# Products with moving weights: columns read in turn from two halves of a weight row

## The reference

```
h = rmsnorm(x, g)                                  # 256 x 1024
proj = h @ w_in                                    # 1024 x 6672, split: q, k, v, gates, ...
mixed = gs0 * (ya @ w_branch_a) + gs1 * (yb @ w_branch_b) + gs2 * (yc @ w_branch_c)
x = x + rmsnorm(mixed @ w_out, g)
f = (silu(h @ w_gate) * (h @ w_up)) @ w_down       # 1024 x 2816, twice, and 2816 x 1024
...                                                # three such feed-forward layers in all,
                                                   # a second mixer, a cross attention to 256 memory rows
```

## Time and profile before

| what | value |
|---|---|
| median of three runs | 1101.3 us (1101.09 to 1101.75) |
| span of the profiled execution | 1100.8 us |
| TensorE matmul busy | 1087.9 us, 99% |
| TensorE weight load busy | 981.1 us, 89% |
| VectorE busy | 719.8 us, 65% |
| ScalarE busy | 555.3 us, 50% |
| DMA, mean over the span | 192 GB/s |

### The profile page before, as it was taken

One profiled execution on the slowest core, in us unless ns is written; L12 is line 12 of the kernel. 1 busy time (PEld: TensorE's weight loads), 2 busy tenths in 40 slices (PEclk: granted clock), 3 DMA queues, 4 the chain that ended last, 5 costly groups with the idle time before them and its releaser, 6 DMA issues.

```text
span 1100.8 us, 18185 instructions
## 1 busy us (share of the span) xinstructions
PE 1087.9 (99%) x7530; PEld 981.1 (89%) x7530; DVE 719.8 (65%) x1085; ACT 555.3 (50%) x840; POOL 30.3 (3%) x49
## 2 busy tenths in 40 slices
PE   9999999999999999999999999999999999999997
PEld 8898878889999988899999889887788989999985
DVE  5687665877666645656666545867767657666653
ACT  6643575545444544544454445646644446445442
POOL 0000500000000000000000001000000000000000
PEclk9999999999999999999999999999999999999999
DMA  7654545655665665576686559534365445565662
GB/s 265 231 173 159 192 148 198 225 188 175 193 204 185 221 200 182 192 248 211 233 274 207 174 186 321 185 113 128 122 235 173 148 133 188 189 202 190 196 203 77
DMA packets 63821, 211.01 MB, mean 192 GB/s; under 512 B 7451, under 2 KB 14803, under 8 KB 62844
## 3 DMA queue, kind: packets, MB, share of 16 engines
q1 hardware_dynamic: 63452, 209.57, 57.6%
q10 hardware_dynamic: 288, 0.29, 0.1%
HBM read 206.41 MB, written 5.27 MB: 192 GB/s over the span
## 4 chain that ended last, share of the span: by engine, by line
PE 85%; DVE 6%; ACT 4%; DMA 3%; issue 1%; POOL 0%; SPq 0%; POOLq 0%; ACTq 0%; DVEq 0%
PE ps L869 13%; PE ps L872 13%; PE ps L871 13%; PE ps L861 12%; PE ps L863 12%; PE ps L862 12%; DMA raw<-in_wflat 3%; DVE wlo L1652 1%; PE ps L911 1%; ACT whi L1313 1%; PE ps L1043 1%; PE ps L958 1%; ACT m_Pb L1463 1%; PE ps L1029 1%; PE ps L1234 1%
## 5 line engine op out<-in xcount | busy, mean ns | idle before, releaser
L869 PE MATMUL ps<-hT_hi,whi_b 128*128 128x256 f32 x1344 | 373.7, 278 | 0.5 <-DVE wlo_b L1652 0.5
L871 PE MATMUL ps<-hT_hi,wlo_b 128*128 128x256 f32 x1344 | 371.2, 276 | 0.0
L872 PE MATMUL ps<-hT_lo,whi_b 128*128 128x256 f32 x1344 | 371.2, 276 | 0.0
L1652 DVE TENSOR_TENSOR wlo<-raw,whi 128x1024 fp32r<-128x1024 f32 x176 | 215.4, 1240 | 113.7 <-ACT whi L1313 112.9
L1652 DVE TENSOR_TENSOR wlo_b<-raw,whi_b 128x1024 fp32r<-128x1024 f32 (+1 forms) x186 | 217.4, 1189 | 106.2 <-ACT whi_b L1313 105.9
L869 PEld LDWEIGHTS ps<-hT_hi,whi_b 128*128 128x128 f32 x1344 | 252.3, 188 | 3.7 <-issue 2.3
L871 PEld LDWEIGHTS ps<-hT_hi,wlo_b 128*128 128x128 f32 x1344 | 252.3, 188 | 0.3
L872 PEld LDWEIGHTS ps<-hT_lo,whi_b 128*128 128x128 f32 x1344 | 252.3, 188 | 0.0
L1313 ACT ACTIVATE whi<-raw 128x1024 fp32r<-128x1024 f32 x176 | 181.9, 1057 | 110.4 <-PE ps L863 89.1
L1313 ACT ACTIVATE whi_b<-raw 128x1024 fp32r<-128x1024 f32 (+1 forms) x186 | 183.2, 1024 | 32.4 <-PE ps L863 15.3
L861 PE MATMUL ps<-whi,hT_hi 128*128 128x512 f32 (+1 forms) x256 | 101.8, 398 | 1.6 <-DVE wlo L1652 1.6
(11 more groups left out here) (338 smaller groups left out, 1317.6 us busy)
## 6 DMA issues: line engine op xcount, KB each, us to landing
raw<-in_wflat SPq DMA_DIRECT2D x355, 512.0 KB, 4.0
wide<-scratch SPq DMA_DIRECT2D x1, 2048.0 KB, 11.2
m_w<-in_cmp_k_w SPq DMA_DIRECT2D x4, 512.0 KB, 6.1
m_w<-in_cmp_v_w SPq DMA_DIRECT2D x4, 512.0 KB, 6.1
m_alibi<-in_c_alibi SPq DMA_DIRECT2D x1, 1536.0 KB, 6.6
m_xT<-in_xT SPq DMA_DIRECT2D x4, 256.0 KB, 5.6
x<-in_x SPq DMA_DIRECT2D x2, 512.0 KB, 8.9
m_memT<-in_memT SPq DMA_DIRECT2D x1, 1024.0 KB, 5.9
```

What stands on the lines that cost most here:

```text
L869: e.matmul(o, hi[:, k, c], xs.h(k0 + k), start=first and k == 0 and f % 2 == 0, stop=False, skip_group_check=True)
L871: e.matmul(o, lo[:, k, c], xs.h(k0 + k), start=False, stop=False, skip_group_check=True)
L872: r = e.matmul(o, hi[:, k, c], xs.l(k0 + k), start=False, stop=last and k == kt - 1, skip_group_check=True)
L1652: e.tensor_tensor(slot(wlo, u)[:, w], raw[u % NRAW][:, w], slot(whi, u)[:, w].bitcast(F32), ALU.subtract).then_inc(*w_lo.did(u, c))
```

## The change

A helper gives an access pattern that reads the first half and the second half of a row in turn: word 0, word n/2, word 1, word n/2 + 1, and so on. All moving weight operands of kind "a" go through it. The host lays the columns of these products out as all even ones and then all odd ones, so that what is read in turn is the original order of columns, and results and evictions stay as they were. Kinds "b" and "s" and everything else are untouched.

```
+        def in_turn(ap):
+            return ap.rearrange("p (a b) -> p b a", a=2)
...
-                            e.matmul(o, xh, hi[:, k, :], start=first and k == 0, stop=False)
-                            e.matmul(o, xh, lo[:, k, :], start=False, stop=False)
-                            r = e.matmul(o, xl, hi[:, k, :], start=False, stop=last and k == kt - 1)
+                            e.matmul(o, xh, in_turn(hi[:, k, :]), start=first and k == 0, stop=False)
+                            e.matmul(o, xh, in_turn(lo[:, k, :]), start=False, stop=False)
+                            r = e.matmul(o, xl, in_turn(hi[:, k, :]), start=False, stop=last and k == kt - 1)
...
-                        e.matmul(o, xh, h[:, k, :], start=False, stop=False)
-                        e.matmul(o, xh, l[:, k, :], start=False, stop=False)
-                        r = e.matmul(o, xl, h[:, k, :], start=False, stop=v == u and j == last and k == kt - 1)
+                        e.matmul(o, xh, in_turn(h[:, k, :]), start=False, stop=False)
+                        e.matmul(o, xh, in_turn(l[:, k, :]), start=False, stop=False)
+                        r = e.matmul(o, xl, in_turn(h[:, k, :]), start=False, stop=v == u and j == last and k == kt - 1)
...
         w = np.concatenate([np.asarray(inputs[n])[0][:, cols] for n in ws], 1)
+        if PRODUCTS[name][0] == "a":
+            w = np.concatenate([w[:, 0::2], w[:, 1::2]], 1)
```

## The result

The change made the kernel **faster, by 1.7%**: the median of four runs is 1082.39 us (1080.58 to 1084.71) against 1101.19 us for the kernel before (four runs), a ratio of 0.9826 with a 95% interval of 0.9809 to 0.9844. The forecast was 1235 us; the measured time is near the 1078.7 that rival 1 gave; some 4 us of the gain that it named are missing. The profiled execution after took 1084.7 us with a span of 1082.8, so about 1.9 us lie around a span. (By the same 1.9 us the profiled execution before, with its span of 1100.8, took some 1102.7, and not 1101.3; this is an estimate.

What follows compares the result with a forecast made beforehand. TensorE's matmul steps were taken to bound the kernel; 2088 x 0.0635 + 48 x 0.0318 = +134 us on the 1100.8 us span, and 0.5 us to the median, gave 1235 us. Own range 1150 to 1540; 8-in-10 range 1072 to 1540.

Steps and rivals of the forecast that it cites:

- rival 1: Weight-moving matmuls: neighbours' collision costs one clock in 16, two separated streams avoid it; 1078.7 us, down to 1073; chance 0.29.
- What bounds the kernel: TensorE, busy 98.9% of 1100.8 us: time is about the sum of steps between matmul starts; 2088 changed ones take 0.2267 us each.
- 2088 x s: The whole effect: a surcharge s on each of 2088 matmuls of 512 columns, plus 48 x s / 2; either sign.
- The surcharge s: Added time per 512-column matmul for reading in turn: +63.5 ns on 226.7 ns, giving +134 us in all.
- the row that is nearest in form: VectorE's line 1867, alternating between two rows: 0.28 of an element's time, carried to TensorE as 63.5 ns a matmul.
- The prices of the upper ends: Larger surcharges on the changed matmuls, from VectorE's rows or a second clock: +317 to +865 us, 1418 to 1966 us.
- A second clock per column: Each column of the changed matmuls needs its own fetch: 432 ns for 512 columns, +434 us, 1535 us.
- Its cover: For rival 1: a unit falls to 2.59 us against VectorE's 1.22, loads would need 202 GB/s, so other engines keep up.

Runs made afterwards that it cites:

- run 1: Changed kernel, but the 512 columns read in turn from four quarters of a row, 512 bytes apart, host layout to match: 1213.78 us.
- run 8: Changed kernel, but the weights read as one stream with a step of four words, 16 bytes: 1591.96 us.
- run 10: Changed kernel, but two streams in turn from the two halves, each with a step of two words (A0, B0, A2, B2): 1101.2 us.
- run 5: Changed kernel, but the two streams in turn only 16 bytes apart (words 0, 4, 1, 5, 2, 6, 3, 7): 1082.19 us.
- run 9: Changed kernel, but words read as 0, 2, 1, 3, then 4, 6, 5, 7, turns at 8 bytes: 1101.34 us.
- run 3: Changed kernel, but pairs in turn, two neighbouring words from the first half, then two from the second: 1326.75 us.

## Why the prediction was wrong

**What bounds the kernel: right, with a gap.** The counts and the steps before held. That the whole effect is 2088 x s held for three quarters: 2088 x -11.6 ns are -24.2 us, and the span shrank by 18.0.

**The surcharge s: wrong in sign, and this is the step that failed.** I took +63.5 ns from line 1867, "the row that is nearest in form", and it was -11.6. The step that failed is carrying a price of VectorE's reads over to TensorE's: a reading in turn cost VectorE 75 ns for 256 elements in that row, and it took away TensorE's one lost clock in 16. The trace held a hint in the pace itself: a plain float32 stream of line 1234 gives each column two clocks and loses next to nothing, and the float32r stream loses one clock in 16 in strict proportion to the columns, so there was something to gain. I wrote both down, for rival 1, and gave a faster kernel 0.29. Jumps do cost TensorE dearly in other orders, by the picture above when a reader has fewer than two uses of a line in a row: with four quarters in turn the kernel took 1214 us, near the 1235 that I gave for two. The forecast fits a neighbour of the change.

**The prices of the upper ends.** A second clock per column, 432 ns, was the right scale for a step of two or four words (451 and 461 ns, 1574 and 1592 us); it was simply not this change.

**Rival 1: right in time, wrong in reason.** It said 216 ns a step and 1078.7 us, by a collision of neighbouring columns that separation avoids. The step was right to the nanosecond; in runs 1, 8 and 10 every column lies in another 16-byte line than the one before, and they take 283, 461 and 226.7 ns, so separation by itself does nothing. Turns helped just when each parity of columns walks through neighbouring words, four to a line. Its cover was judged too kindly: "with TensorE hardly waiting now" overlooked that in several stretches VectorE had only just kept up. In the profiled execution they took back some 5 us in waits, and half clock 1.7; in the trace of run 5, waits alone, 3.0.

**Two rules against the trace.** The rule of the Trainium skill, page "SBUF — State Buffer", the note on cachelines in its section on the DMA port swizzle, asks for two hits on a 16-byte line. Taken of the stream of columns, it spoke against the change; the sum took no term from it, and the measurement decides. Taken of each parity of columns, it orders nine of the eleven patterns: one hit 451 and 461 ns, two hits 226.7 (nearly the full rate), four hits 215.8. It fails for pairs in turn and four quarters in turn, which have one hit at a time and take 340 and 283. The Trainium skill, page "TensorE: Matmul & The Clock Gate", section "Back-to-back issue gap", gives N/2.4 + 2.5 ns, 215.8 ns for 512 columns. The turns reach just that; the contiguous float32r stream of this kernel takes 226.7.

**What stays open.** Two readers are a picture that foretold runs 9 and 10; no row shows a reader. It doesn't give the prices where a reader goes to and fro between two lines. Per group of eight columns, pairs in turn take 340 / 64 = 5.31 ns, three openings of 1.77, where one buffer would make four and two buffers two; per sixteen columns, four quarters take 283 / 32 = 8.85 ns, five openings, where one buffer would make eight. I have no account for three and five, and they describe the commonest steps alone (run 3 has many of 327 to 336 ns, run 1 some of 270 to 276). Nor was it tried whether the start of an operand within its 16 bytes matters.

## What to carry to other kernels

Where float32r matmuls run back to back on the full clock, divide the distance between their starts by the columns: 0.443 ns instead of 0.421 is the mark of this loss. Let the moving operand be read as two interleaved contiguous runs (a distance of 16 bytes is enough, so the permutation can stay within eight words), lay weights out for it on the host, and let elementwise stages carry activations in the order read. A step of two words in a float32r moving operand doubled the time here. And before pricing a shorter step, look for the stretches where another engine has only just kept up: they give part of it back.

## What the runs showed that was not expected

- A moving float32r operand read with a step of two words costs 451 ns for 512 columns, of four words 461, though the first finds two of its columns in each 16-byte line and the second one; read in turn at any distance from 16 to 1024 bytes it costs 215.8, contiguous 226.7.
- Reading in turn at 8 bytes (0, 2, 1, 3) costs 226.7 ns, just as contiguous.
- With 256 columns read in turn and 128 stationary columns per matmul, the step doesn't go below 111.7 ns; with 16 or 32 stationary columns it is 109.
- A stationary operand with a step of two words lengthens its load from 189 to 196 ns, hidden behind 512 columns.
